# Splitting weight tiles in pairs in a two-layer fp32 kernel

## The reference

```
u = rmsnorm(h);  proj = u @ w_in                       # 2048 x 4096
h = h + concat(fourier_mix, dilated_attention) @ w_out # 2048 x 2048
h = h + square(relu(rmsnorm(h) @ w_up)) @ w_down       # 2048 x 8192 x 2048
# second layer: modulation vectors from silu(c) @ w_mod (12288 of them, for two c)
z  = modulated_norm(h or ctx) @ w_in_2                 # feeds GLA and mLSTM scans
x  = x + gate * merge(heads) @ w_out_2
x  = x + gate * (silu(conv3x3(u_gate)) * u_val) @ w_down_2   # u = norm(x) @ w_up_2
return rmsnorm(x)
```

## Time and profile before

| | us |
|---|---|
| median of 3 runs | 2348.55 (2347.39 to 2348.67) |
| profiled execution | 2347.09 |
| its span in the profile | 2345.3 |

### The profile page before, as it was taken

The page is one execution under the profiler, slowest core; times in us unless marked ns, Lnnn a source line. Parts: engine busy times, 40 slices in busy tenths (PEclk is TensorE's granted clock), DMA queues, the critical chain, the costliest instruction groups (busy, mean ns, idle before and its releaser), DMA issues.

```text
span 2345.3 us, 31050 instructions
## 1 busy us (share of the span) xinstructions
PE 2322.2 (99%) x12026; PEld 1972.4 (84%) x12026; DVE 1682.7 (72%) x2096; ACT 1141.9 (49%) x1418; POOL 0.2 (0%) x4
## 2 busy tenths in 40 slices
PE   8999999999999999999999999999999999999998
PEld 7888888888888888888888888788888888888887
DVE  5445778878868868657667754886788658875786
ACT  5444645445435435647355453764444434443444
POOL 0000000000000000000000000000000000000000
PEclk9999999999999999999999999999999999999999
DMA  8552777877877877667829965084556665555554
GB/s 297 191 194 97 253 253 276 297 285 276 300 279 280 300 284 258 243 177 305 302 75 366 342 215 195 13 323 144 198 188 207 196 206 189 188 194 192 189 185 147
DMA packets 136342, 533.46 MB, mean 227 GB/s; under 512 B 19152, under 2 KB 19536, under 8 KB 122400
## 3 DMA queue, kind: packets, MB, share of 16 engines
q1 hardware_dynamic: 135936, 531.73, 64.1%
q10 hardware_dynamic: 288, 0.11, 0.0%
HBM read 529.67 MB, written 2.11 MB: 227 GB/s over the span
## 4 chain that ended last, share of the span: by engine, by line
PE 94%; DVE 3%; ACT 2%; issue 1%; DMA 0%; DVEq 0%; ACTq 0%
PE PSA L812 23%; PE PSA L655 18%; PE PSA L657 18%; PE PSA L656 18%; PE PSA L808 6%; PE PSA L815 6%; PE PSA L856 1%; DVE wlo L2003 0%; ACT whi L1330 0%; DVE u L2157 0%; PE PSA L757 0%; PE PSA L896 0%; PE PSA L1001 0%; PE PSA L945 0%; PE PSA L924 0%
## 5 line engine op out<-in xcount | busy, mean ns | idle before, releaser
L2003 DVE TENSOR_TENSOR wlo<-raw,whi 128x1024 fp32r<-128x1024 f32 x788 | 933.9, 1219 | 341.6 <-ACT whi L1330 340.2
L1330 ACT ACTIVATE whi<-raw 128x1024 fp32r<-128x1024 f32 x788 | 799.8, 1052 | 472.0 <-DMA raw<-in_w_down 175.4
L812 PE MATMUL PSA<-u,whi 128*128 128x512 f32 x2368 | 566.1, 391 | 0.0
L812 PEld LDWEIGHTS PSA<-u,whi 128*128 128x128 f32 x2368 | 435.1, 188 | 84.2 <-DVE u L2157 0.2
L655 PE MATMUL PSA<-whi,u 128*128 128x512 f32 x1088 | 426.0, 392 | 3.6 <-DVE wlo L2003 3.6
L657 PE MATMUL PSA<-whi,u 128*128 128x512 f32 x1088 | 423.6, 389 | 0.0
L656 PE MATMUL PSA<-wlo,u 128*128 128x512 f32 x1088 | 423.5, 389 | 0.0
L655 PE MATMUL PSA<-whi,ahi 128*128 128x512 f32 x856 | 333.9, 390 | 0.0
L657 PE MATMUL PSA<-whi,alo 128*128 128x512 f32 x856 | 333.1, 389 | 0.0
L656 PE MATMUL PSA<-wlo,ahi 128*128 128x512 f32 x856 | 333.1, 389 | 0.0
L655 PEld LDWEIGHTS PSA<-whi,u 128*128 128x128 f32 x1088 | 204.3, 188 | 47.7 <-issue 3.4
(11 more groups left out here) (336 smaller groups left out, 1296.4 us busy)
## 6 DMA issues: line engine op xcount, KB each, us to landing
raw<-in_w_up SPq DMA_DIRECT2D x300, 512.0 KB, 3.4
raw<-in_w_in SPq DMA_DIRECT2D x208, 512.0 KB, 4.0
mod_slot<-in_w_mod_rows SPq DMA_DIRECT2D x96, 1024.0 KB, 5.8
raw<-in_w_down SPq DMA_DIRECT2D x192, 512.0 KB, 3.4
raw<-in_w_out SPq DMA_DIRECT2D x64, 512.0 KB, 3.5
raw<-in_w_down2b SPq DMA_DIRECT2D x20, 512.0 KB, 3.7
c_all<-in_c_rows SPq DMA_DIRECT2D x3, 1024.0 KB, 4.8
xc<-in_ctx SPq DMA_DIRECT2D x2, 1024.0 KB, 5.8
```

Of the source, the lines that this page charges most:

```text
L812: mm = pe.matmul(both, wh[:, c], u_pair[:, k, :], start=k == 0, stop=k == KD - 1)
L1330: AF(whi[:, n % SLOTS, 0:w], raw[:, n % SLOTS, 0:w], ACT.Copy).then_inc(hi_done, 1)
L2003: TT(wlo[:, n % SLOTS, 0:w], raw[:, n % SLOTS, 0:w], whi[:, n % SLOTS, 0:w], ALU.subtract).then_inc(lo_done, 1)
```

## The change

Outside the first block of the first iteration of each stage, two neighbouring tiles (t even and t + 1, which lie in neighbouring slots) are split by one instruction on each engine: ScalarE waits for both loads and copies 2048 columns, VectorE waits until both are counted and subtracts 2048 columns; each then counts 2 on its semaphore. In dn2_2, the last pair of a block has 1536 columns. The pair stands where the split of the even tile stood; the work placed between the two tiles' splits now follows the pair. The first block keeps single splits. TensorE, SyncE and the ring are unchanged.

```diff
+            def split_pair(p, i, b, t):              # ScalarE
+                n = p.main_at(b, t)
+                w = 2 * TW
+                if p.k == 11 and t == p.per_block - 2:
+                    w = TW + NBLK
+                for m in (n, n + 1):
+                    act.wait_ge(arrived[m % SLOTS], p.plus_tiles(16 * (m // SLOTS + 1), i, 2))
+                pair = slice(n % SLOTS, n % SLOTS + 2)
+                AF(whi[:, pair, :].rearrange("p s c -> p (s c)")[:, 0:w], raw[:, pair, :].rearrange("p s c -> p (s c)")[:, 0:w], ACT.Copy).then_inc(hi_done, 2)
...
+            def split_pair(p, i, b, t):              # VectorE
+                n = p.main_at(b, t)
+                w = 2 * TW
+                if p.k == 11 and t == p.per_block - 2:
+                    w = TW + NBLK
+                pair = slice(n % SLOTS, n % SLOTS + 2)
+                dve.wait_ge(hi_done, p.main0 + b * p.per_block + t + 2 + i * p.per_iter)
+                low, full, high = (x[:, pair, :].rearrange("p s c -> p (s c)")[:, 0:w] for x in (wlo, raw, whi))
+                TT(low, full, high, ALU.subtract).then_inc(lo_done, 2)
...
-                            if not (isinstance(i, int) and i == 0 and b == 0 and t < early):
-                                split(p, i, b, t)
+                            if isinstance(i, int) and i == 0 and b == 0:
+                                if t >= early:
+                                    split(p, i, b, t)
+                            elif t % 2 == 0:
+                                split_pair(p, i, b, t)
```

## The result

The changed kernel takes 2364.02 us (median of 4 runs, 2363.21 to 2364.75) against 2348.22 us for the kernel before in the same series: a ratio of 1.0066, 95% interval 1.0055 to 1.0078, or 15.8 us more. The profiled execution has a span of 2361.4 us, 16.1 more than before.

A forecast was written before the change was run, and what follows sets the result against it. TensorE, busy 99% of the span, was taken as the bound. Losses of 3.9 us (up1 and dn1), 2.0 (inC) and 0.45 (in1) summed to 6.35 us, giving 2354.9 us from 2348.55, range 2350.0 to 2358.5.

The forecast's parts named there:

- All else I take as zero: All places outside up1 with dn1, inC's gates and in1: no loss, with bounds from -0.7 to +1.0 us.
- Price of a pair: Length of one joint split: 1.92 us on ScalarE, 2.29 us on VectorE.
- Rival four: A pair saves nothing (2.00 us on ScalarE, 2.44 on VectorE), giving 2363.0 us; chance 0.04.
- The up1 loop: In up1, the ScalarE-VectorE loop grows from 22.35 to 22.95 us; waits in up1 and dn1 cost 3.9 us.
- Rival one: In up1 the cushions hold, so the 3.9 us go and 2.45 remain: 2351.0 us; chance 0.16.
- rival two: Saved start costs pay, VectorE dropping 0.26 us per block; at most 1.9 us come back: 2346.7 us; chance 0.04.
- Rival five: Pairs change nothing measured, since eight slots hide them everywhere: 2348.6 us; chance 0.05.
- The gates of inC: Around inC block (0,1), a pair delays the sum LA and the split behind the gates: 2.0 us lost.
- in1: In in1 block (0,1), the first pair ends after TensorE asks for its weights: 0.45 us lost.
- Both tiles of a pair were there: Both tiles' loads have arrived when ScalarE starts a pair, read from seven gapless splits from 572.36.
- rival three: Mod buffers freed later hold SyncE's load queue, 1 us in each of 12 paired up1 blocks: 2366.9 us; chance 0.04.
- TensorE's own busy time must not change, or none of this holds: Sign for the whole kernel: TensorE's busy time stays the same; if it changes, the prediction doesn't hold.

The follow-up runs named there:

- e2: Changed kernel, but tiles 4 and 5 of the paired up1 blocks split singly (12 of 313 pairs): 2355.45 us, ratio 1.0033 to the kernel before.
- e5: Changed kernel, but only ScalarE splits in pairs; VectorE uses two single instructions behind each: 2356.82 us, ratio 1.004 to the kernel before.
- e6: Changed kernel, but ScalarE splits the two tiles singly and VectorE jointly behind both: 2361.42 us, ratio 1.0059 to the kernel before.
- e1: Changed kernel, but stage out2 split singly: 2357.16 us, ratio 1.0043 to the kernel before.
- the repeat: The changed kernel run again unaltered, beside the other follow-up runs: 2362.35 us, ratio 1.0062 to the kernel before.
- e9: Changed kernel, but two pairs of inC split singly, one ahead of the sum LA, one behind the gates: 2359.12 us, ratio 1.005 to the kernel before.
- e3: Changed kernel, but stages dn1_3, inC and inL split singly: 2356.82 us, ratio 1.0038 to the kernel before.
- e8: Changed kernel, but each joint split replaced by two single instructions in its place, behind the same joint waits: 2349.08 us, ratio 1.0006 to the kernel before.
- e7: Changed kernel, but one pair split singly, tiles 0 and 1 of out2 block (0,1): 2360.02 us, ratio 1.0056 to the kernel before.

## Why the prediction was right or wrong, point by point

The direction was right, the size wrong: 2354.9 us predicted (range 2350.0 to 2358.5), 2364.0 measured. In the traces 16.1 us were added where the sum had 6.35. The step that failed is the term "All else I take as zero": it measured 6.9 us, 5.2 of them in out2. The remaining 2.8 us are two terms with the right mechanism and too small a size, inC (1.5) and up1 (1.2), and the scatter of the start.

- **Price of a pair: right.** 1.91 us on ScalarE (1.92 taken), 2.29 on VectorE (2.29). Rival four fell with it; that its 2363.0 us is within 1 us of the result is luck.
- **The up1 loop: right in mechanism, a quarter too small.** rl is spaced 23.00 us where 22.95 was worked out, VectorE idles 5.18 us where 5.1 was. The stalls are 0.55 us in the last up1 block (0.39) and 0.94 in dn1 (0.77), together 5.1 us instead of 3.9. The mis-sized term is small and repeated: tile 4 is ready 0.16 us later than the sum gave, 0.10 of it because each of the two lengthened loops is 0.05 longer than assumed, and tile 5 of dn1 0.29. With almost no cushion left, such tenths count in full, seven times. Rival one is dead (e2, e5, e6: three loop lengths, each near the worked-out one), and rival two with it: VectorE comes to the pair 5.2 us early. Rival five, no change, lies far outside the interval.
- **The gates of inC: right in mechanism, too small.** 2.0 us worked out; e1's trace has 2.3, the first trace 3.5, the repeat 3.9. In the repeat TensorE is 6.47 us late when block (0,1) begins. Its gate rows (VectorE, ScalarE, TensorE):

```profile
1074.14 2.35 DVE L2077 TENSOR_TENSOR LA<-PSA,blr 128x1024 f32<-128x1024 f32 x2
...
1086.96 2.31 DVE L2082 SCALAR_TENSOR_TENSOR LA<-LA,TM 128x2064 f32<-128x2064 f32 x1 [4.13 <-ACT TM L1364]
...
1089.46 2.28 DVE L2018 TENSOR_TENSOR wlo<-raw,whi 128x2048 fp32r<-128x2048 f32 x1
...
1076.52 1.93 ACT L1360 ACTIVATE TM<-LA 128x2064 f32<-128x2064 f32 x1 [4.51 <-DVE LA L2077]
...
1091.80 0.64 PE L655 MATMUL PSA<-whi,u 128*128 128x512 f32 x1 [2.87 <-DVE wlo L2018]
```

  LA is 1074.14 - 1066.21 - 6.47 = 1.46 us late (1.20 worked out), the gates 1.26 (0.95), the tile behind them 2.3 (2.0). The remaining 1.6 us of the repeat are the clock (last section). In the first trace the remainder is another thing: the splits of this stage already ran 1.2 us later than in the repeat, and tile 6 of (0,1) gave a stall of its own of 0.9 us. e9 confirms the place: two pairs, 3.5 us.
- **in1: right.** The step at in1 (0,1) is 0.50 us (0.46 to 0.52 in the traces that split this block in pairs on both engines), against 0.45.
- **"All else I take as zero": wrong, and the largest error.** out1 0.2, dn1_3 1.0, out2 5.2 (3.2 in the repeat), dn2_2 0.8, less 0.3 that inL gives back: 6.9 us, where the bounds ended at +1.0. The prediction did name out1, dn1_3, out2 and the start of dn2_2 as near the limit, but compared the slack of their tiles with one pair's length (1.1 or 1.9 us). The slack of a tile is eaten by every pair between it and the last point at which the engines were synchronised with TensorE: in out2 the silu, the sum h and the split behind it fall 3.3, 4.1 and 5.1 us behind TensorE, and tile 4 is ready 6.1 behind, where it had 2.9 us to spare (ready at 1555.14, first matmul at 1558.00 before).
- **"Both tiles of a pair were there": wrong where it mattered.** It was read from seven splits in one up1 block and used for every stage. In out2 ScalarE waits 7.62 and 9.87 us for the load in front of a pair. The earlier trace rows already listed 471.6 us of such waits. In dn1_3 the pair of tiles 0 and 1 of (0,1) waits for its load too; the stalls follow at tiles 2 and 4. The load stands behind SyncE's xc loads, which wait for VectorE's last mod sums (7.6 us instead of 4.4) and are issued 8.6 us later than before (934.73 there) while TensorE is 5.9 us late. Changed kernel, ScalarE and SyncE's queue:

```profile
961.58 1.92 ACT L1332 ACTIVATE whi<-raw 128x2048 fp32r<-128x2048 f32 x1 [1.59 <-DMA raw<-in_w_down]
...
943.32 0.80 SPq L504 DMA_DIRECT2D xc<-in_ctx  x2
```

  This is rival three's mechanism, late buffers that hold the load queue, in two stages instead of twelve blocks. Its price was wrong (2366.9 was close to the result by chance, since none of its 12 us arose in up1); the share of it that exists is dn1_3's 1.0 us, and a part of out2's that the runs don't separate from the pair's length. e3 and e8 limit it. In e3 the second load of dn1_3 (0,1) lands as late as in the changed kernel (962.03 and 961.47), and with single splits the stage adds 0.1 us; in e8 the second load of out2 (0,1) lands 0.9 us behind its place, as in the repeat, and out2 adds nothing.
- **"TensorE's own busy time must not change, or none of this holds": a bad test.** It rose by 6.3 us with the granted clock at 0.999 in both traces; stalls leak into it, as shown above.
- **The rule of the skill.** The Trainium skill, "Perfetto Trace Analysis", section "Optimizing Scalar/DVE Operations", says that breaking instructions up may complete work sooner where an engine isn't saturated but makes bubbles elsewhere. The runs agree with this half: VectorE at 70% gained nothing from 18.0 us less work, and e8, the same order and waits with broken-up instructions, takes back all but 1.2 us. The other half, the gain of a saturated engine, no run here can show.

## What to carry to other kernels

Joining two operations of a producer that is not the bottleneck saves its own time and delays the hand-over of the first half; with both engines in series joint, the delay is paid on each (0.86 and 1.07 us here), and where the engines run in a closed loop, as in up1, it adds up from turn to turn. Before such a change, don't compare one tile's slack with one instruction's length: follow each stage from the last point where the producer waited for the bottleneck, and count every joint instruction up to the tightest tile. If the saving isn't needed, as here, join nothing; if it is, leave single the few pairs in front of something that another engine waits for (here some 20 of 313 made nearly the whole cost).

## What the hardware showed that was not expected

The granted clock of TensorE fell behind a stall of about 3 us, in some executions and not in others. Stretches of the repeat (first three) and of the first trace of the changed kernel (last), behind the gates of inC; the columns are us, busy time and count of each engine, granted clock, share of the transfer engines, GB/s:

```profile
1080.00:1088.50 8.50, 8.50 (x39) 7.06 (x38) 3.83 (x2) 8.44 (x6) 0.00 (x0) 1.00 0.09 35
1088.50:1091.80 3.30, 0.43 (x2) 0.01 (x2) 3.27 (x5) 2.68 (x4) 0.00 (x0) 1.00 0.38 84
1091.80:1095.20 3.40, 3.40 (x8) 2.68 (x9) 3.40 (x3) 0.44 (x1) 0.00 (x0) 0.53 0.99 412
```

```profile
1093.40:1096.80 3.40, 3.40 (x15) 2.80 (x16) 3.40 (x3) 0.44 (x1) 0.00 (x0) 1.00 1.01 418
```

Behind 2.87 us of waiting the repeat's clock is 0.53, about the lower level of 1.2 GHz instead of 2.4, and 8 matmuls run where 15 do at 1.00; they start 0.43 us apart instead of 0.23, which costs 1.6 us. Behind 3.15 us of waiting the first trace shows no fall at all. Behind 2.7 to 3.05 us e2, e6 and e7 show one (7, 12 and 7 matmuls), e1, behind 2.9, doesn't. So the length of the stall alone doesn't decide it in these traces, and what does is open. A stall of this length had a second price of 0 to 2.4 us that varied with the execution. The 3.8, 3.9 and 5.2 us of e2, e7, the repeat and e6 in row inC contain it, the changed kernel's 3.5 and e1's 2.3 don't. e2 has a second such stretch from 1625.4 to 1629.0 (granted clock 0.56), within the 1.1 us of row up2_0.
